# State-space sums of a two-layer block: the time step moves into the exponent, whole causal blocks are exponentiated straight from the rows, and a half chunk of the weight stream runs ahead of each head

## The reference, cut to what matters

```python
A_cs = jnp.cumsum(A, axis=2)
seg = A_cs[:, :, :, None] - A_cs[:, :, None, :]
Lmat = jnp.exp(jnp.where(tri, seg, -jnp.inf))
CB = jnp.einsum("bclgn,bcsgn->bclsg", Cc, Bc)
Y_diag = jnp.einsum("bclsgr,bcsgrp->bclgrp", CB[..., None] * Lmat, X)
```

## Time and profile before

| | |
|---|---|
| Median of 3 runs | 2431.92 us (2431.38 to 2432.03) |
| The profiled execution, its own time | 2432.59 us |
| Its span, first to last instruction | 2430.8 us |
| Mean granted TensorE clock | 0.983 |
| PE matmul busy | 2336.9 us, 96% |
| DVE busy | 1583.1 us, 65% |
| ACT busy | 1078.1 us, 44% |
| POOL busy | 448.9 us, 18% |
| The state-space stage, first CB to last sums | 1327.9 to 1533.5 us |

### The profile page before, as it was taken

One profiled execution on the slowest core, in us unless ns is written; L12 is line 12 of the kernel. 1 busy time (PEld: TensorE's weight loads), 2 busy tenths in 40 slices (PEclk: granted clock), 3 DMA queues, 4 the chain that ended last, 5 costly groups with the idle time before them and its releaser, 6 DMA issues.

```text
span 2430.8 us, 43347 instructions
## 1 busy us (share of the span) xinstructions
PE 2336.9 (96%) x18663; PEld 2233.0 (92%) x18663; DVE 1583.1 (65%) x2636; ACT 1078.1 (44%) x1491; POOL 448.9 (18%) x306
## 2 busy tenths in 40 slices
PE   6999999999999999999998999996999999999998
PEld 6999999999899999999997777896999998888998
DVE  3446565554564666699999888695756446666564
ACT  3335555544443554334344444443545344444443
POOL 6210000000000000378773000760000012221000
PEclk9999999999999999999998999998999999999999
DMA  7765445555565565545553354455555556555652
GB/s 226 173 106 174 149 147 159 173 163 188 156 191 182 182 187 161 165 139 174 174 173 124 116 150 141 137 159 150 173 174 173 166 174 174 149 156 157 191 177 102
DMA packets 392559, 394.00 MB, mean 162 GB/s; under 512 B 27237, under 2 KB 386133, under 8 KB 391925
## 3 DMA queue, kind: packets, MB, share of 16 engines
q1 hardware_dynamic: 373984, 383.22, 51.7%
q0 software_dynamic: 1904, 2.82, 1.3%
q10 hardware_dynamic: 16480, 5.19, 0.9%
HBM read 388.85 MB, written 5.95 MB: 162 GB/s over the span
## 4 chain that ended last, share of the span: by engine, by line
PE 86%; DVE 9%; ACT 2%; issue 1%; DMA 1%; ACTq 1%; SPq 0%; DVEq 0%; PEldq 0%
PE ps L422 25%; PE ps L424 24%; PE ps L423 24%; PE ps L2326 3%; DVE ps L1654 3%; PE ps L2393 1%; DVE arena L1763 1%; DVE wlo L375 1%; PE ps L2370 1%; PE ps L2382 1%; PE ps L2153 1%; DMA raw<-in_w_in_dram 1%; PE ps L2170 1%; ACTq L1066 1%; PE ps L2072 1%
## 5 line engine op out<-in xcount | busy, mean ns | idle before, releaser
L422 PE MATMUL ps<-op_hi,whi 128*128 128x256 f32 (+1 forms) x5440 | 1573.7, 289 | 17.2 <-DVE wlo L375 7.5
L424 PE MATMUL ps<-op_hi,wlo 128*128 128x256 f32 (+1 forms) x5440 | 1555.6, 286 | 0.0
L423 PE MATMUL ps<-op_lo,whi 128*128 128x256 f32 (+1 forms) x5440 | 1553.0, 285 | 0.0
L368 ACT ACTIVATE whi<-raw 128x1024 fp32r<-128x1024 f32 (+1 forms) x688 | 720.6, 1054 | 944.1 <-PE ps L424 902.0
L422 PEld LDWEIGHTS ps<-op_hi,whi 128*128 128x128 f32 x5440 | 1031.8, 190 | 52.6 <-issue 48.4
L424 PEld LDWEIGHTS ps<-op_hi,wlo 128*128 128x128 f32 x5440 | 1032.4, 190 | 0.0
L423 PEld LDWEIGHTS ps<-op_lo,whi 128*128 128x128 f32 x5440 | 1030.4, 189 | 0.2
L375 DVE TENSOR_TENSOR wlo<-raw,whi 128x1024 fp32r<-128x1024 f32 x552 | 667.8, 1227 | 505.1 <-ACT whi L368 504.5
L375 POOL TENSOR_TENSOR wlo<-raw,whi 128x1024 fp32r<-128x1024 f32 x136 | 336.3, 2483 | 1156.8 <-ACT whi L368 1156.5
L1654 DVE SCALAR_TENSOR_TENSOR ps<-arena,param_cols,ps 128x257 f32<-128x257 f32 (+6 forms) x448 | 183.4, 488 | 0.6
L734 POOL TENSOR_TENSOR arena<-arena 128x256 f32<-128x256 f32 x64 | 64.7, 1032 | 275.8 <-DMA arena<-bias_by_column 275.8
(11 more groups left out here) (346 smaller groups left out, 1450.3 us busy)
## 6 DMA issues: line engine op xcount, KB each, us to landing
raw<-in_e_w_in_dram SPq DMA_DIRECT2D x96, 1024.0 KB, 5.4
raw<-in_w_in_dram SPq DMA_DIRECT2D x84, 1024.0 KB, 5.2
raw<-in_o_w_in_dram SPq DMA_DIRECT2D x64, 1024.0 KB, 6.1
raw<-in_e_w_out_dram SPq DMA_DIRECT2D x32, 1024.0 KB, 5.3
raw<-in_w_out_dram SPq DMA_DIRECT2D x16, 1024.0 KB, 5.3
raw<-in_w_ple_gate_dram SPq DMA_DIRECT2D x16, 1024.0 KB, 5.3
raw<-in_o_w_out_dram SPq DMA_DIRECT2D x16, 1024.0 KB, 5.3
arena<-cum_rows SPq DMA_DIRECT2D x16, 544.0 KB, 6.1
```

Of the source, the lines that this page charges most:

```text
L368: nc.scalar.activation(half_view(whi[c % 2], c, n), half_view(raw[c % RING], c, n), ACT.Copy).then_inc(hi_ready, 1)
L422: nc.tensor.matmul(o, wh, xh, start=(i % cpp == 0 and k == 0), stop=False)
L423: nc.tensor.matmul(o, wh, xl, start=False, stop=False)
L424: mm = nc.tensor.matmul(o, wl, xh, start=False, stop=(i % cpp == cpp - 1 and k == 7))
```

## The change

Four things are changed.

1. The logarithm of dt is taken once (ACT, under `gg`, after a clamp by DVE), and kept in `dtN`'s place as `LND`; `cN` becomes `LNB`, which is log dt minus the cumulative sum.
2. A weight is now exp(row + LNB) times CB. `weigh` needs no time step and becomes two plain products of 800 and 288 columns instead of six; `SSD_COLS` gets places that make this possible.
3. The blocks that lie wholly on the causal side (128 and 144 columns on 128 rows, 256 columns on 16 rows) no longer pass through `seg`. ACT reads them from `ROWS` with `LNB` as bias. The diagonal blocks still go through `seg`, that of tile 1, forward, with the 16 whole columns behind it. `seg` keeps six instructions, now with two column operands each, on 560 instead of 1088 columns.
4. On PE each head's sums have one half chunk ahead of them. Half 0 of the next group's first chunk moves from ahead of CB to ahead of head 3's sums; in the last group it is half 0 of `z2`'s chunk 0.

```diff
-SSD_COLS = [(0, 0, 0, T2, 0), (0, 1, P, T2, 272), (1, 0, 0, P, 416), (1, 1, 0, 2 * P, 544),
-            (0, 2, 2 * P, T2, 800), (1, 2, 0, T2, 816)]
+SSD_COLS = [(0, 0, 0, T2, 528), (0, 1, P, T2, 384), (1, 0, 0, P, 256), (1, 1, 0, 2 * P, 0),
+            (1, 2, 0, T2, 800), (0, 2, 2 * P, T2, 1072)]
...
+            def gg_extra(i):
+                gg_sigmoid(i)
+                if i == 4:
+                    act.wait_ge(S("a_nat_ready"), 1)
+                    nc.scalar.activation(LND[:, :, :], sp[5], ACT.Ln).then_inc(S("sp_exp"), 1)
...
-                        nc.scalar.activation(SEG[:, h % 2, 0:800], SEG[:, h % 2, 0:800], ACT.Exp)
-                        nc.scalar.activation(SEG[0:META, h % 2, 800:1088], SEG[0:META, h % 2, 800:1088], ACT.Exp).then_inc(S("seg_exp"), 1)
+                        sg, rw = SEG[:, h % 2], ROWS[:, h // 2, :, h % 2, :]
+                        nc.scalar.activation(sg[:, P:656], sg[:, P:656], ACT.Exp)
+                        nc.scalar.activation(sg[:, 656:800], rw[:, 0, P:T2], ACT.Exp, bias=LNB[:, 0, 4 * G + h:4 * G + h + 1])
+                        nc.scalar.activation(sg[:, 0:P], rw[:, 1, 0:P], ACT.Exp, bias=LNB[:, 1, SH + 4 * G + h:SH + 4 * G + h + 1])
+                        nc.scalar.activation(sg[0:META, 800:1056], rw[0:META, 1, 0:2 * P], ACT.Exp,
+                                             bias=LNB[0:META, 2, SH + 4 * G + h:SH + 4 * G + h + 1])
+                        nc.scalar.activation(sg[0:META, 1056:1088], sg[0:META, 1056:1088], ACT.Exp).then_inc(S("seg_exp"), 1)
...
+                v.do(V.tensor_scalar(sp[5], dtN[:, :, :], 1e-38, None, ALU.max))
...
-            v.do(V.tensor_copy(cN[:, 0:2, :], ps[:, 4, 0:128].rearrange("p (a n) -> p a n", a=2)))
-            v.do(V.tensor_copy(cN[0:META, 2, :], ps[0:META, 4, 128:192]))
+            dve.wait_ge(S("sp_exp"), 3)
+            v.do(V.tensor_tensor(LNB[:, 0:2, :], LND[:, 0:2, :], ps[:, 4, 0:128].rearrange("p (a n) -> p a n", a=2), ALU.subtract))
+            v.do(V.tensor_tensor(LNB[0:META, 2, :], LND[0:META, 2, :], ps[0:META, 4, 128:192], ALU.subtract))
...
-                for i, (d, st, lo, hi, at) in enumerate(SSD_COLS):
+                for d, st, lo, hi, at in SSD_COLS:
                     n = P if st < 2 else META
-                    ins = V.tensor_scalar(SEG[0:n, b, at:at + hi - lo], ROWS[0:n, hp, d, h % 2, lo:hi],
-                                          cN[0:n, st, ds(G * 4 + (SH * d + h), 1)], 0.0, ALU.subtract, ALU.min)
+                    f = (P * st, P * st + n) if hi - lo > P + META else (lo, hi)
+                    col = ds(G * 4 + (SH * d + h), 1)
+                    ins = V.tensor_scalar(SEG[0:n, b, at + f[0] - lo:at + f[1] - lo], ROWS[0:n, hp, d, h % 2, f[0]:f[1]],
+                                          LNB[0:n, st, col], LND[0:n, st, col], ALU.add, ALU.min)
...
-                for i, (d, st, lo, hi, at) in enumerate(cols):
-                    n = P if st < 2 else META
-                    sg = SEG[0:n, b, at:at + hi - lo]
-                    ins = V.scalar_tensor_tensor(out=sg, in0=sg, scalar=dtN[0:n, st, ds(G * 4 + (SH * d + h), 1)],
-                                                 in1=CBM[0:n, at:at + hi - lo], op0=ALU.mult, op1=ALU.mult)
+                for n, lo, hi, last in ((P, 0, 800, 3), (META, 800, 1088, 5)):
+                    if SSD_COLS[last] in cols:
+                        sg = SEG[0:n, b, lo:hi]
+                        ins = V.tensor_tensor(sg, sg, CBM[0:n, lo:hi], ALU.mult)
...
+            def beside(i, n):
+                if i < s.chunks:
+                    multiply(pe, s, i, n, T2)
+                else:
+                    multiply(pe, ST["z2"], 0, n, T2)
...
-                    multiply(pe, s, 2 * G, 0, T2)
+                    if G == 0:
+                        multiply(pe, s, 0, 0, T2)
...
-                        for i in {0: (1,), 2: (2, 3)}.get(h, ()):
-                            multiply(pe, s, 2 * G + i // 2, i % 2, T2)
+                        beside(2 * G + (h + 1) // 2, (h + 1) % 2)
...
-            stream_pe(pe, "z2", NT=T2)
+            multiply(pe, ST["z2"], 0, 1, T2)
+            stream_pe(pe, "z2", NT=T2, lo=1)
```

More of the change, by code:

```diff
@@ L263, in build @@
         dtN = sb("dt_nat", [P, 3, 2 * SH])
+        LND = dtN
         cN = sb("cum_nat", [P, 3, 2 * SH])
+        LNB = cN
         sp = [ar(15240 + 192 * i, 3, 2 * SH) for i in range(6)]
@@ L989, in h2s_early @@
                         split_op_act(act, "h2s", op(H2S, T2), op(MH, T2), 4, ST["gg"].end - 1, only=gq)
-            side("gg", pre=h2s_early, extra=gg_sigmoid)
+            def gg_extra(i):
[3 more added lines that the diff above has]
+                    nc.scalar.activation(LND[:, :, :], sp[5], ACT.Ln).then_inc(S("sp_exp"), 1)
+            side("gg", pre=h2s_early, extra=gg_extra)
             for gq in range(2, 4):
```

## The result

| | before | changed |
|---|---|---|
| Median | 2431.65 us (2429.34 to 2432.03) | 2473.31 us (2467.60 to 2473.55) |
| Ratio, 95% interval | | 1.0168 (1.0156 to 1.0180) |
| The profiled execution, its own time | 2432.59 us | 2473.06 us |
| Its span | 2430.8 us | 2471.3 us |
| Mean granted TensorE clock | 0.983 | 0.980 |

The change costs 41.7 us by the medians and 40.5 by the spans of the two profiled executions. DVE has 21 us less to do, and the kernel is slower. The place is the state-space stage: its first CB starts at 1327.9 and 1328.0, and the second half of `z2`'s first chunk, the first work that lies behind the stage in both orders, starts at 1578.20 us where it started at 1538.90: 39.3 us later. The remaining 1.2 us lie behind it.

What follows compares the result with a forecast made beforehand. PE's own work bounds a group (23.81 of 24.95 us busy); the new order adds waits for DVE's chains. Terms of +27 us and +10 for the clock, on 2432.6, gave 2469.6, forecast as 2469 (2450 to 2482).

Steps and rivals of the forecast that it cites:

- The bound: Plain group: PE busy 23.81 of 24.95 us, so lighter DVE or ACT work can gain about 1.1 us, nothing more.
- The exponentials: ACT's exponentials: 1.65 us a head against 1.11 before, lying beside DVE's work; otherwise at most 0.5 us per group.
- Head 0's wait: PE asks for head 0 after 6.4 us, DVE's chain takes 9.1: wait 2.7 us where it was 0.4.
- Head 2's: PE's wait before head 2's sums: DVE's chain 5.2 to 5.3 us against a 3.1 us half chunk, 2.1 us.
- A group without a fall: Plain group's time from the two new waits, without clock loss: 24.95 - 0.4 + 2.7 + 2.1 = 29.4 us.
- Group 0: First group: only head 2's wait and one more half chunk inside it (3.1 us), +5 us.
- `z2`'s first half: Work behind the last sums: the first half of z2's stream is already done, -5.6 us.
- The clock: Lower granted clock after PE's waits: 1.4 us once per group in groups 1 to 7, +10; bounds 0 and +20.
- Group 7: Last group, POOL beside DVE: PE waits 3.7 us instead of 2.1, group 31.0 us against 30.33, +0.7.
- `weigh` 2 takes 5.2 us: Last group: weighing head 2 beside POOL is slowed 3.6 times, to 5.2 us.
- the waits leave the clock alone: Rival, 33%: PE's new waits don't lower the granted clock; +27 us, 2459.
- The half chunks do hide DVE's work: Rival, 7%: the chain behind the weights is ready at 6.4 us, half chunks cover the rest; -9 us, 2424.

Runs made afterwards that it cites:

- e9: Changed kernel with PE's old order, third CB tile mid half chunk, ACT's head 0 exponentials before its copy, low parts after head 0's weighing: 2418.78 us.
- e11: As e9, but DVE weighs head 1 before it makes the low parts: 2418.19 us.
- e7: Changed kernel with only the low parts ahead of head 0's chain (chunk 2G+3) moved behind head 0's weighing: 2450.11 us.
- e3: Changed kernel with DVE weighing head 2 before it makes the low parts of chunk 2G+2: 2454.31 us.
- e1: Kernel before with PE's new matmul order alone, old arithmetic: 2469.08 us.
- e4: Changed kernel with both DVE moves, head 2 weighed before its low parts and the other low parts made after head 0's weighing: 2434.78 us.
- e5: Changed kernel with the diagonal blocks clamped at constant 0 instead of the log dt column, which computes something else where dt is over 1: 2455.92 us.
- e2: Changed kernel with PE's old matmul order, so the new arithmetic alone: 2423.57 us.
- e8: As e4, with DVE instead of POOL making the low parts of z2's first two chunks: 2427.95 us.
- e13: Repeat of e1, the kernel before with PE's new matmul order alone: 2469.79 us.

## Why the prediction was right

2469 was forecast with a range of 2450 to 2482; 2473.31 was measured. Slower by more than 0.2% had 91%. The mechanism, two waits of PE for DVE's chains, is right; two terms of the sum came out near for other reasons than given, and one was wrong.

- **The bound.** A plain group of before has 1.1 us of idle time, and that much and "nothing more" was said to be open to gain. This nearly holds: the arithmetic alone gave 0.26 us, e9 0.58, e11 1.16. But PE's own work wasn't fixed: in e11 it is busy for 23.54 us instead of 23.81, so 0.27 of the 1.16 come from there.
- **`seg`** was put at 1.47 us; it takes 1.51, with 339 ns for 128 columns where the row said 344. **`weigh`** was put at 1.28 and takes 1.34. **The exponentials** were put at 1.65 and take 1.76 where DVE is not in their way:

```profile
1433.74 0.65 ACT L1038 ACTIVATE arena<-arena 128x528 f32<-128x528 f32 x1 [5.36 <-DVE arena L1768]
...
1435.29 0.21 ACT L1043 ACTIVATE arena<-arena 16x32 f32<-16x32 f32 x1
```

- **`gg`** was put at +0.3; the first CB starts 0.08 us later than before.
- **Head 0's wait:** 2.7 forecast, 2.53 measured. **Head 2's:** 2.1 forecast, 2.00 measured. Heads 1 and 3: none, as forecast. Undoing each wait alone (e7, e3) took 2.27 and 2.06 us off a group, so these two waits are shown to be the loss.
- **A group without a fall:** 29.4 forecast, 29.6 measured. It came so near in part by luck. The wait of before was taken as 0.4 us, where its own row says 0.16; the new waits were put 0.27 too long; and the rise of PE's own busy time by 0.28 us (0.45 for the order, less 0.17 for the shorter sums) was put at nothing.
- **Group 0:** +5 forecast, +5.1 measured. **`z2`'s first half:** -5.6 forecast; between the last sums and the second half the distance shrank by 5.5. (The window of 5.63 us ends two matmuls into the second half.)
- **The clock:** 1.4 us once per group in groups 1 to 7. Groups 1 to 6 have five falls, of 1.35 to 1.6 us, 7.3 together where 8.4 was forecast. The size is right by luck: the reason given, that a wait near 2.3 us brings the clock down and a shorter one doesn't, is not borne out. e1 has waits of 2.99 and 2.56 and no fall, twice, and in group 3 of the changed kernel the fall comes with the wait of 2.00, not with that of 2.53.
- **Group 7** is the term that was wrong: +0.7 and 1.4 for the clock, against +4.4 measured. The step that failed is "`weigh` 2 takes 5.2 us" beside POOL. `weigh` fell between POOL's two pairs and was not slowed (1.34 us); `seg` of head 3 was, from 1.51 to 4.66 us. The 5.2 also has a slip: 3.6 times the 1.28 of the sum is 4.6, and the group would be at +0.1. And the price was a factor, where the trace shows a number of instructions that wait: three in the 10.29 us of before, at some 2.1 us each ((10.29 - 3.89) / 3), two here. The prediction set a rule of the Trainium skill aside (GPSIMD Engine Reference, Specifications: GpSimd's SBUF interface is shared with VectorE, and a two-port instruction contends too). The trace agrees that `seg` is held up beside POOL; that its ports are the reason no run shows. The 2.4 us that were put beside the rule stand against 3.1 here and 4.2 in e4. With a wait of 2.87 us and 10.2 us at the lower clock, the group is the costliest of the eight.

Added up: 0.1 + 5.1 + 35.2 (six groups, the falls among it) + 4.4 - 5.5 = 39.3, against 37 forecast. Against the forecast the falls are 1 us less, group 7 is 2.3 us more, and six groups at 29.6 in place of 29.4 make most of the rest.

Of the rivals, *the waits leave the clock alone* (2459) has fallen for the changed kernel as profiled, but it is what groups 1 to 6 of e5, e7 and e1 did. *The half chunks do hide DVE's work* fell at the point named: the chain is 9.1 us long, not 6.4.

The two parts of the change pull against each other. In the new order the lighter arithmetic takes a group from 30.8 to 29.6 us, some 7 us over six groups; in the profiled executions the five falls that come with the new pattern take 7.3 back. So the order alone and the whole change end within 5 us of each other.

## What to carry to other kernels

Before work is spread evenly over a queue, count for each consumer the time from its producer's last release to its own request, on both sides: here even spacing cut PE's cover for head 0 from 9.5 to 6.4 us, against a chain of 9.1, and took half of head 2's. It also made PE itself busy for some 0.4 us more a group. The cheaper order was the old one with the producer's non-urgent work (low parts) moved behind the urgent, and with the consumer's single wait filled from the work right behind it. And a gain per iteration has to be checked in the iteration that has other neighbours: the last group took 3.7 to 7.8 us more than a plain one in e4, e5, e7 and e11, and POOL works in no other.

## What was not expected of the hardware

- A second column operand costs a subtraction some 60 ns (e5), over a quarter of its whole time at 16 columns (217 ns); the row of before had said 67.
- POOL's subtractions don't slow DVE's instructions by a factor. Single instructions of DVE wait until one of POOL's has ended, and the rest run at their usual speed. Two of the six in `seg` did (1.51 to 4.66 and 5.71 us), and of four in `weigh` two in e2 and e9 (2.61 to 7.00 and 6.98 us) and three in e11 (9.19). It also goes the other way: in e9 a POOL instruction takes 3.48 us instead of 2.4, with a DVE product of 0.97 inside it. e8 shows that POOL is the cause. That the two take turns by whole instructions is read from the traces, and which of them goes first was not tested.
- Whether the granted clock falls to 1.2 GHz is not told by the length of PE's wait alone. In the profiled executions waits of 2.53 and 2.00 us brought five falls of 3.4 us in six groups, one of 2.53 alone (e3) brought three of 6.8 us, 2.99 with 2.56 (e1, e13) and 2.00 with 0.26 (e7) brought none. The Trainium skill (TensorE: Matmul & The Clock Gate, Part 1) says that the number of matmuls at the lower clock varies between runs of one kernel. In groups 1 to 6 two profiled executions of each of two kernels show no such variation; ahead of the stage they do (3.9 us in the start of the first CB of the changed kernel), and the eight times of the changed kernel, 2464.61 to 2474.43 at mean clocks of 0.980 to 0.984, fit it as well. What in the pattern decides stays open.
